# Hybrid decoder layer on one core: the second part of queries and keys in all attention scores on 128 rows

## What is computed

```python
h = modulate(rms_norm(x, norm_mix), sh2, sc2)
cq, ckv, kr, q_n, k_n, v_n, g_n = split_cols(h @ w_in, IN_SPLITS)   # 768, 512, 64, 8*192, 6*192, 6*128, 24
o_mla = mla_group(cq, ckv, kr, ...)      # 8 heads: q, k = 128 + 64 columns (the 64 with rope), v = 128
o_nsa = nsa_group(q_n, k_n, v_n, ...)    # 8 heads in 2 groups, q and k of 192 columns, v of 128
x += g2 * concat([o_mla, o_nsa]) @ w_out
```

## Time and profile before

| | |
|---|---|
| three runs | 2255.92 us median (2254.13 to 2256.14) |
| profiled execution, from its first to its last instruction | 2253.2 us |
| the runs above that span | 0.9 to 2.9 us |
| PE busy | 95% of the span |
| DVE, ACT, POOL busy | 61%, 41%, 2% |
| mean granted clock of PE | 0.973 of 2.4 GHz |
| attention, first score to last exponential | 1253.3 to 1363.9 us, 110.6 us |

### The profile page before, as it was taken

One profiled execution on the slowest core, in us unless ns is written; L12 is line 12 of the kernel. 1 busy time (PEld: TensorE's weight loads), 2 busy tenths in 40 slices (PEclk: granted clock), 3 DMA queues, 4 the chain that ended last, 5 costly groups with the idle time before them and its releaser, 6 DMA issues.

```text
span 2253.2 us, 28432 instructions
## 1 busy us (share of the span) xinstructions
PE 2151.5 (95%) x9352; PEld 1656.4 (74%) x9352; DVE 1383.9 (61%) x1839; ACT 921.0 (41%) x1150; POOL 41.7 (2%) x55
## 2 busy tenths in 40 slices
PE   6976999999999999899999999989999999999997
PEld 1344888888887787788856777878888888877776
DVE  4645667776778888776635456466775444444444
ACT  2223444444433333444433344444444544434332
POOL 0010000000000000000003100000000000000000
PEclk9997999999999999999999789999999999999999
DMA  8976777877878889687777312548786656656553
GB/s 314 315 210 204 269 271 263 292 264 262 277 270 294 310 320 335 190 288 259 249 211 253 113 38 69 193 137 282 257 293 201 183 176 188 185 173 204 186 184 130
DMA packets 272859, 513.18 MB, mean 228 GB/s; under 512 B 15954, under 2 KB 31485, under 8 KB 272417
## 3 DMA queue, kind: packets, MB, share of 16 engines
q1 hardware_dynamic: 270888, 508.37, 67.4%
q10 hardware_dynamic: 1913, 4.06, 0.9%
HBM read 508.50 MB, written 3.87 MB: 227 GB/s over the span
## 4 chain that ended last, share of the span: by engine, by line
PE 92%; DMA 4%; DVE 2%; issue 1%; ACT 1%; ACTq 0%; POOL 0%; DVEq 0%; SPq 0%
PE ps L597 27%; PE ps L598 27%; PE ps L599 27%; PE ps L635 2%; PE ps L838 2%; DMA bias_by_distance<-rev_sb 2%; DMA ada_raw<-in_w_ada_dram 1%; PE ps L961 1%; PE ps L959 1%; PE ps L997 1%; PE ps L679 1%; DMA ada_raw<-in_w_cmp_k_dram 1%; PE ps L626 1%; PE ps L653 1%; PE ps L982 1%
## 5 line engine op out<-in xcount | busy, mean ns | idle before, releaser
L1389 DVE TENSOR_TENSOR w_lo<-raw,w_hi 128x1024 fp32r<-128x1024 f32 (+1 forms) x657 | 790.9, 1217 | 432.8 <-ACT w_hi L1087 428.6
L1087 ACT ACTIVATE w_hi<-raw 128x1024 fp32r<-128x1024 f32 (+1 forms) x657 | 687.2, 1055 | 797.8 <-PE ps L599 558.2
L597 PE MATMUL ps<-w_hi,hT_hi 128*128 128x512 f32 (+1 forms) x1856 | 743.4, 401 | 39.8 <-ACT silu_gate L1093 28.4
L598 PE MATMUL ps<-w_lo,hT_hi 128*128 128x512 f32 (+1 forms) x1856 | 734.8, 396 | 0.0
L599 PE MATMUL ps<-w_hi,hT_lo 128*128 128x512 f32 (+1 forms) x1856 | 734.4, 396 | 0.0
L597 PEld LDWEIGHTS ps<-w_hi,hT_hi 128*128 128x128 f32 x1856 | 351.8, 190 | 133.5 <-issue 39.5
L599 PEld LDWEIGHTS ps<-w_hi,hT_lo 128*128 128x128 f32 x1856 | 351.7, 189 | 84.4
L598 PEld LDWEIGHTS ps<-w_lo,hT_hi 128*128 128x128 f32 x1856 | 352.1, 190 | 81.9 <-issue 1.0
L1408 DVE SCALAR_TENSOR_TENSOR ada_acc<-ada_raw,silu_c,ada_acc 128x512 f32<-128x512 f32 x476 | 358.4, 753 | 33.7 <-DMA ada_raw<-in_w_ada_dram 24.4
L597 PE MATMUL ps<-w_hi,actT_hi 128*128 128x512 f32 x704 | 283.7, 403 | 3.4 <-DVE silu_gate L1524 3.4
L598 PE MATMUL ps<-w_lo,actT_hi 128*128 128x512 f32 x704 | 279.0, 396 | 0.0
(11 more groups left out here) (195 smaller groups left out, 1047.4 us busy)
## 6 DMA issues: line engine op xcount, KB each, us to landing
ada_raw<-in_w_ada_dram SPq DMA_DIRECT2D x288, 512.0 KB, 4.9
raw<-in_w_gate_dram SPq DMA_DIRECT2D x176, 512.0 KB, 4.1
raw<-in_w_up_dram SPq DMA_DIRECT2D x176, 512.0 KB, 4.7
raw<-in_w_down_dram SPq DMA_DIRECT2D x176, 512.0 KB, 4.6
raw<-in_w_in_dram SPq DMA_DIRECT2D x72, 512.0 KB, 4.7
raw<-in_w_out_dram SPq DMA_DIRECT2D x32, 512.0 KB, 4.4
raw<-in_w_uq_dram SPq DMA_DIRECT2D x9, 512.0 KB, 5.6
ada_raw<-in_w_cmp_k_dram SPq DMA_DIRECT2D x8, 512.0 KB, 7.6
```

The lines of the kernel that those rows point to most:

```text
L597: pe.matmul(bank, lhs_hi, rhs_hi, start=start, stop=False)
L598: pe.matmul(bank, lhs_hi, rhs_lo, start=False, stop=False)
L1087: act.activation(part(U, w_hi, s), part(U, raw, s), ACT.Copy).then_inc(hi_done, 1)
L1389: dve.tensor_tensor(part(U, w_lo, s), part(U, raw, s), part(U, w_hi, s).bitcast(F32), ALU.subtract)\
```

## The change

The second part of every score becomes a product over 128 rows, of which 64 rows of the keys are zero. For an NSA head the stationary operand is the query's last 64 columns and the 64 columns after them; for an MLA head it is the last 128 of the head's 192 columns, so that the rope columns are rows 64 to 127. POOL sets the zero halves by three memsets, and PE waits for them once before attention. The two ACT copies of an NSA query become one of 128x512. The sizes of all other work stay.

```diff
-            krT = sb("krT", [ROPE, SEQ], within=s)
+            krT = sb("krT", [P, SEQ], within=s)
...
-            kT64 = sb("kT64", [ROPE, 6, SEQ], within=s)
+            kT64 = sb("kT64", [P, 6, SEQ], within=s)
...
-            kc64 = sb("kc64", [ROPE, GROUPS * N_CMP], within=s)
+            kc64 = sb("kc64", [P, GROUPS * N_CMP], within=s)
...
-            qrT = sb("qrT", [ROPE, 2, SEQ], within=s)
+            qrT = sb("qrT", [P, 2, SEQ], within=s)
...
+            pool.wait_ge(mm_done, Unit("dn0", D // CW - 1).done(KF // 2 - 1))
+            pool.memset(kT64[ROPE:P], 0.0).then_inc(A["pads_set"], 1)
+            pool.memset(kc64[ROPE:P], 0.0).then_inc(A["pads_set"], 1)
+            pool.wait_ge(mm_done, Unit("win", STAGES["win"][0] - 1).done(KD // 2 - 1))
+            pool.memset(krT[0:ROPE], 0.0).then_inc(A["pads_set"], 1)
+            pool.wait_ge(A["pads_set"], 3)
             for r in range(5):
                 round_lo("mla", r, cqT if r < 3 else ckvT, 2 * r if r < 3 else 2 * r - 6)
...
-                mm = pe.transpose(ps[0:ROPE, T_BANK, t * P:(t + 1) * P], proj[:, t, C_KR:C_KR + ROPE], ident[:, :])
+                mm = pe.transpose(ps[:, T_BANK, t * P:(t + 1) * P], proj[:, t, C_KR - ROPE:C_KR + ROPE], ident[:, :])
             mm.then_inc(A["kr_turned"], 1)
             pe.wait_ge(A["kc_copied"], 2)
             pe.wait_ge(A["vc_copied"], 2 * HPG)
+            pe.wait_ge(A["pads_set"], 3)
...
-                        mm = pe.transpose(ps[0:ROPE, T_BANK, cols2], proj[:, t, q0 + NOPE:q0 + DK], ident[:, :])
+                        mm = pe.transpose(ps[:, T_BANK, cols2], proj[:, t, q0 + NOPE:q0 + NOPE + P], ident[:, :])
...
-                        mm = pe.transpose(ps[0:ROPE, T_BANK + 1, cols], q_mla[:, t, h * DK + NOPE:(h + 1) * DK],
-                                          ident[:, :])
+                        mm = pe.transpose(ps[:, T_BANK + 1, cols], q_mla[:, t, (h + 1) * DK - P:(h + 1) * DK], ident[:, :])
...
-                    mm = pe.matmul(dst, qrT[:, b, t * P:(t + 1) * P],
-                                   kT64[:, kx, 0:w] if nsa else krT[:, 0:w], start=False, stop=True)
+                    q_rope = qkT[:, b, SEQ + t * P:SEQ + (t + 1) * P] if nsa else qrT[:, b, t * P:(t + 1) * P]
+                    mm = pe.matmul(dst, q_rope, kT64[:, kx, 0:w] if nsa else krT[:, 0:w], start=False, stop=True)
...
-                        mm = pe.matmul(dst, qrT[:, b, t * P:(t + 1) * P], kc64[:, g * N_CMP:(g + 1) * N_CMP],
-                                       start=False, stop=True)
+                        mm = pe.matmul(dst, qkT[:, b, SEQ + t * P:SEQ + (t + 1) * P],
+                                       kc64[:, g * N_CMP:(g + 1) * N_CMP], start=False, stop=True)
...
-            act.activation(krT[:, :], ps[0:ROPE, T_BANK, 0:SEQ], ACT.Copy).then_inc(A["kr_copied"], 1)
+            act.activation(krT[ROPE:P, :], ps[ROPE:P, T_BANK, 0:SEQ], ACT.Copy).then_inc(A["kr_copied"], 1)
...
-                if nsa:
-                    act.activation(qkT[:, e % 2, 0:SEQ], ps[:, T_BANK, 0:SEQ], ACT.Copy)
-                    act.activation(qrT[:, e % 2, :], ps[0:ROPE, T_BANK, SEQ:2 * SEQ], ACT.Copy)\
-                       .then_inc(A["qk_copied"], 1)
-                else:
-                    act.activation(qkT[:, e % 2, :], ps[:, T_BANK, :], ACT.Copy).then_inc(A["qk_copied"], 1)
+                act.activation(qkT[:, e % 2, :], ps[:, T_BANK, :], ACT.Copy).then_inc(A["qk_copied"], 1)
...
-                    dve.tensor_copy(qrT[:, e % 2, :], ps[0:ROPE, T_BANK + 1, 0:SEQ]).then_inc(A["qr_copied"], 1)
+                    dve.tensor_copy(qrT[:, e % 2, :], ps[:, T_BANK + 1, 0:SEQ]).then_inc(A["qr_copied"], 1)
```

More of the change, by code:

```diff
@@ L362, in decoder_layer @@
                                  "cmp_turned", "cmp_copied", "cmp_pv", "cmp_o", "cmp_w_landed",
-                                 "rope_landed")}
+                                 "rope_landed", "pads_set")}
         final_done, final_b_landed, stored = sem("final_done"), sem("final_b_landed"), sem("stored")
@@ L1663, in copy_rope_keys @@
                 dve.wait_ge(A["k_turned"], r + 1)
-                dve.tensor_copy(kT64[:, 2 * r:2 * r + 2, :].rearrange("p k n -> p (k n)"), ps[0:ROPE, KEY_BANK[r] + 1, :])\
+                dve.tensor_copy(kT64[0:ROPE, 2 * r:2 * r + 2, :].rearrange("p k n -> p (k n)"), ps[0:ROPE, KEY_BANK[r] + 1, :])\
                    .then_inc(A["kT64_copied"], 1)
@@ L1685, in _ @@
             dve.wait_ge(A["kT64_copied"], 1)
-            add_position(1, ROPE, kpe64, lambda g: kT64[:, g, :])
+            add_position(1, ROPE, kpe64, lambda g: kT64[0:ROPE, g, :])
             copy_rope_keys(2)
@@ L1718, in copy_keys @@
                 dve.tensor_copy(kc128[:, :], ps[:, 5, 0:n]).then_inc(A["kc_copied"], 1)
-                dve.tensor_copy(kc64[:, :], ps[0:ROPE, 5, 32:32 + n]).then_inc(A["kc_copied"], 1)
+                dve.tensor_copy(kc64[0:ROPE, :], ps[0:ROPE, 5, 32:32 + n]).then_inc(A["kc_copied"], 1)
             def copy_values():
```

## The result

The changed kernel took 2224.5 us (median of 4 runs, 2220.6 to 2231.2) against 2255.0 for the kernel before (2251.7 to 2256.1). The ratio is 0.988, with a 95% interval of 0.985 to 0.991. The forecast was 2225.5, in a range of 2218 to 2240.

The account below looks back on a forecast made before the run. PE, busy 95% of the span, was taken to bound the kernel. Savings of 20.1 us to unit 9's maxima, 2.3 before MLA, 7.4 in MLA steps and 0.6 at the end make 30.4: 2255.9 to 2225.5 us, range 2218 to 2240.

Parts of the forecast that it names:

- The stall and its price: PE's scores and transposes: time is lost where 64 and 128 rows alternate; 0.72 us per unit, 24 units.
- steps 4 to 9: NSA part of attention: DVE's row maxima, not PE, set the pace, at 3.17 us a step.
- the ring: Steps 10 to 13: maxima, exponentials, probabilities copy, w_hi, w_lo, next maxima; no PE work, so it keeps 17.45 us.
- the four steps: Steps 10 to 13, from unit 9's row maxima to unit 13's: 17.45 us before, forecast unchanged.
- Rival D: Attention: DVE and ACT loops are shorter than read, PE alone decides; 37.9 us saved, 2218.0 us; chance 0.05.
- The wait before step 16: Before the first MLA query: PE still waits 1.90 us, then one fall of the clock costing 1.7 us.
- unit 13's maxima: DVE's row maxima ending steps 10 to 13; from there to the first MLA query 4.85 us instead of 7.11.
- The clock: PE in steps 1 to 15: 2.4 GHz but for short falls, as row changes no longer stall NSA steps.
- Rival A: Attention: stalls go but the clock stays as it was; 17.8 us saved, 2238.1 us; chance 0.17.
- PE's idle time: PE in attention: idle time grows from 2.7 us to over 10.
- The small edits: Copies and memsets: nothing counted; POOL's 1536-column memset about 1.4 us, a 128-partition query copy 12 ns more on ACT.
- Rival B: Attention: faster PE waits more and stays at 1.2 GHz; slower, 2286.9 us; chance 0.04.

Follow-up runs that it names:

- e1: Changed kernel with the second part of MLA scores back on 64 rows, NSA and compressed scores still on 128: 2231.9 us, ratio 0.992.
- e4: Kernel before with only the single 128x512 ACT copy per NSA query, all second parts still on 64 rows: 2256.3 us, ratio 1.001.
- e5: Changed kernel with ACT's w_hi rounding moved ahead of the exponentials in steps 10 to 13: 2220.8 us, ratio 0.986.
- e10: The changed kernel run again, unaltered, five runs on another chip: 2227.3 us, ratio 0.9885.
- e9: Kernel before with one ACT copy per NSA query and only the compressed scores' second part on 128 rows: 2243.7 us, ratio 0.996.
- e3: Changed kernel with the second part of NSA and compressed scores on 96 rows instead of 128: 2227.2 us, ratio 0.988.
- e6: Changed kernel with w_hi ahead of the exponentials and DVE's reads of the compressed scores one step earlier: 2215.7 us, ratio 0.983.
- e11: The kernel of e6 run again, beside the changed kernel on one chip: 2219.9 us, ratio 0.985.
- e7: Kernel before with the same move of w_hi ahead of the exponentials as e5: 2252.6 us, ratio 1.000.

## Why the prediction was right

**The stall and its price.** Right in kind and size. Priced at 0.22 and 0.44 a pair, the parts take 0.22 and 0.43; the transposes 0.33. e1 to e4 show that it goes with the rows. That 64 rows are slow only where they alternate with more rests on the earlier trace rows alone, whose stationary operands have 30 columns where the scores have 128; a stream of 64-row matmuls with 128 of them was not run. The Trainium skill's rule that few rows cost the same (TensorE: Matmul & The Clock Gate, section Why this matters for your kernels) agrees with the earlier trace rows; for the scores it would have given no gain. The compressed scores were priced at 0.88 and take 0.79.

**What is late next.** Right: DVE sets steps 4 to 9, at 3.11 us a step instead of 3.17; the ring keeps its 17.4 us, and e5 shows that it is the ring. With the ring gone the four steps take 6.2 us less. Rival D, in which PE alone decides, fails on both; its 72.7 us of attention is about what e5 reaches with the ring gone, 73.0.

**The wait before step 16.** 1.90 us as forecast, and one fall of the clock, of 3.41 us, which began in the wait. Against e5, which has none, the MLA steps and the last are 1.3 us longer (28.94 and 27.62), where the sum had 1.7. In e10 the fall lasted 6.8 us and cost 2.9. The stretch from unit 13's maxima was put at 4.85 and took 5.12.

**The clock.** Right that it would recover. The reason given was the changes of rows in the NSA steps, to which the compressed scores add four. e9 shows that the compressed scores are enough to bring the clock back, and leaves open whether their stalls or their rows do it. That steps 1 to 9 passed without a fall was luck in part: e3, e6 and e11 begin with 6.8 us at 1.2 GHz and take 31.7 us to unit 9's maxima, where the sum had 28.7. Rival A would have had attention at 92.8 us; it was 79.9, and 81.5 and 83.6 in e10 and e3.

**PE's idle time.** Wrong: the forecast took every us that DVE and the ring hold PE up for idle time of PE, over 10 us; 79.88 - 74.51 = 5.4 was seen. In steps 1 to 9 the trace counts 28.39 of 28.40 us as busy while the chain runs through DVE. PE's own pace there is 2.98 us a step and DVE's 3.11, and waits of 0.13 us may be lost in the ends of matmuls, which are modelled. In steps 10 to 13 the forecast had 17.45 - 4 x 2.98 = 5.5 us and 2.3 were seen; the 3.4 us at half clock filled part of the wait, the rest is not explained. The sum did not use this number.

**The small edits.** Right. POOL's memset of 1536 columns took 1.37 us (1.4 forecast), beside the same residual:

```profile
912.48 0.69 DVE L1526 TENSOR_TENSOR silu_gate<-ps,gate_b 128x512 f32<-128x512 f32 x1 [0.58 <-PE ps L606]
...
913.84 1.37 POOL L576 MEMSET kT<- 64x1536 f32 x1 [763.37 <-PE ps L606]
```

DVE's copy of a query over 128 partitions takes 422 ns against 416. Rival B, a clock that stays low, did not come.

**The total.** The stages agree to 0.3 us each, more closely than the runs could show: those of the changed kernel spread over 8 to 11 us, those of the kernel before over up to 20. The prediction took its 2 us between runs from three runs alone, which was too narrow. That the median is 1 us from the forecast is partly luck.

## What to carry to other kernels

- Where matmuls with at most 64 rows alternate with matmuls of 128, look at the start-to-start times of each: here a pair or the three transposes took 0.15 to 0.20 us more where the number of rows changed, four times for a score. Rows of zeros, up to 96 or 128 in all, took the stalls away at no price in time that the trace shows.
- When a fix makes one engine faster by a quarter, read the other engines' step lengths first: here a ring through ACT and DVE and a DVE-bound step held back 7.5 of the 37.9 us that, by the forecast's sum, PE alone would have given, and one moved instruction gave back 5.6 of them in the profile.
- Narrow matmuls with few rows can cost more through the clock than through themselves, in a stage that looks fully busy: here about 3 us by their stalls and 8 to 9 by the clock.

## What the runs showed that was not expected

- Eight groups of matmuls of 15 columns, 1.3 us each in 110 us of attention, went with the clock around them: on 64 rows e4's steps 1 to 15 had a mean clock of 0.81, on 128 rows e9's had 1.00, and over ten runs of each the mean clock of the whole is 0.974 and 0.980.
- 96 rows go as 128 do, without a stall.
- The time to the first score moves by 13 us between executions with nearly the same work ahead of it (1249.2 in e6, 1262.5 in e7); PE stood at 1.2 GHz for 54.6 us of it in the first and 71.7 in the second.
